# Hawk and stick-breaking trunk, one core: output projection with residual pieces spread out, one root chain for two token tiles, and another order of its last products

## The reference

```python
h = _rmsnorm(x, a_norm);  proj = h @ a_w_in               # layer 0: recurrent branch and gate, 2560 wide
x = x + (y * silu(gate)) @ a_w_out                        # y: conv, block-diagonal gates, RG-LRU scan
k, v = _rmsnorm(x, kv_norm) @ w_kv                        # shared keys and values
q, gate = _rmsnorm(x, b_norm) @ b_w_in                    # layer 1
o = _stick_breaking_attention(q, k, v)                    # 16 heads of 128
x = x + (o * silu(gate)) @ b_w_out                        # the stage that the change is in
return _rmsnorm(x, final_norm)                            # x * rsqrt(mean(x*x) + 1e-6) * gain
```

## Time and profile before

| | |
|---|---|
| median of three runs | 1665.99 us |
| the profiled execution | 1664.41 us |
| its span, first to last instruction | 1662.7 us |
| granted TensorE clock, mean | 0.998 of full speed |
| PE busy | 1641.9 us, 99% |
| DVE, ACT busy | 1133.9 us (68%), 866.3 us (52%) |
| last matmul starts at | 1650.41 us |

### The profile page before, as it was taken

One profiled execution on the slowest core, in us unless ns is written; L12 is line 12 of the kernel. 1 busy time (PEld: TensorE's weight loads), 2 busy tenths in 40 slices (PEclk: granted clock), 3 DMA queues, 4 the chain that ended last, 5 costly groups with the idle time before them and its releaser, 6 DMA issues. The chain is left out here.

```text
span 1662.7 us, 24345 instructions
## 1 busy us (share of the span) xinstructions
PE 1641.9 (99%) x7479; PEld 1363.8 (82%) x7479; DVE 1133.9 (68%) x1988; ACT 866.3 (52%) x1711; POOL 225.8 (14%) x221
## 2 busy tenths in 40 slices
PE   9999999999999999999999999999999999999997
PEld 8888888888888888888888888888888888887785
DVE  5788887778775545478564666675757666678767
ACT  7655566665565333356555544454554444455555
POOL 0121212122121313120000111011110111010000
PEclk9999999999999999999999999999999999999999
DMA  5556555665433343347666544536353545558765
GB/s 188 176 179 201 167 164 174 202 196 183 146 99 95 105 121 107 119 134 223 206 219 181 166 145 150 188 122 196 114 188 112 187 141 159 173 172 291 248 235 185
DMA packets 216839, 280.81 MB, mean 169 GB/s; under 512 B 16488, under 2 KB 145720, under 8 KB 216760
## 3 DMA queue, kind: packets, MB, share of 16 engines
q1 hardware_dynamic: 212152, 270.05, 51.1%
q10 hardware_dynamic: 4608, 9.83, 1.8%
HBM read 229.09 MB, written 50.72 MB: 168 GB/s over the span
## 5 line engine op out<-in xcount | busy, mean ns | idle before, releaser
L726 PE MATMUL ps<-x_hi,w_hi 128*128 128x512 f32 x1408 | 551.0, 391 | 0.0
L726 PE MATMUL ps<-x_hi,w_lo 128*128 128x512 f32 x1408 | 548.4, 389 | 0.0
L726 PE MATMUL ps<-x_lo,w_hi 128*128 128x512 f32 x1408 | 548.2, 389 | 0.0
L1524 DVE SCALAR_TENSOR_TENSOR w_lo<-stage,cT,w_hi 128x256 fp32r<-128x256 f32 x352 | 192.3, 546 | 284.9 <-ACT w_hi L1064 283.6
L1062 ACT ACTIVATE w_hi<-stage,cT 128x256 fp32r<-128x256 f32 x352 | 178.7, 508 | 374.0 <-PE ps L726 350.0
L726 PEld LDWEIGHTS ps<-x_hi,w_lo 128*128 128x128 f32 x1408 | 264.3, 188 | 55.2
L726 PEld LDWEIGHTS ps<-x_hi,w_hi 128*128 128x128 f32 x1408 | 264.4, 188 | 53.8 <-issue 0.4
L726 PEld LDWEIGHTS ps<-x_lo,w_hi 128*128 128x128 f32 x1408 | 264.4, 188 | 53.7 <-issue 0.2
L1064 ACT ACTIVATE w_hi<-stage,cT 128x256 fp32r<-128x256 f32 x352 | 174.5, 496 | 0.0
L1526 DVE SCALAR_TENSOR_TENSOR w_lo<-stage,cT,w_hi 128x256 fp32r<-128x256 f32 x352 | 172.4, 490 | 0.0
L1521 DVE TENSOR_TENSOR w_lo<-stage,w_hi 128x512 fp32r<-128x512 f32 x100 | 86.9, 869 | 116.5 <-ACT w_hi L1060 116.5
(11 more groups left out here) (253 smaller groups left out, 2579.4 us busy)
## 6 DMA issues: line engine op xcount, KB each, us to landing
stage<-in_a_w_in SPq DMA_DIRECT2D x160, 256.0 KB, 2.8
stage<-in_b_w_in SPq DMA_DIRECT2D x128, 256.0 KB, 2.8
stage<-in_w_kv SPq DMA_DIRECT2D x95, 256.0 KB, 3.0
stage<-in_a_w_out SPq DMA_DIRECT2D x80, 256.0 KB, 2.6
b_raw<-in_w_kv SPq DMA_DIRECT2D x64, 256.0 KB, 3.9
t_scratch<-b_raw SPq DMA_DIRECT2D x64, 256.0 KB, 3.6
wb<-in_b_w_out SPq DMA_DIRECT2D x64, 256.0 KB, 4.7
wt_scratch<-wb SPq DMA_DIRECT2D x64, 256.0 KB, 3.3
```

Source lines behind the costliest of these rows:

```text
L726: mm = pe.matmul(dst, a, b, start=start and n == 0, stop=stop and n == 2, skip_group_check=not check)
L1524: nc.vector.scalar_tensor_tensor(w_lo[:, slot, 0:256], stage[:, slot, 0:256], cT[:, col:col + 1], f(w_hi[:, slot, 0:256]), ALU.mult, ALU.s ...
```

## The change

In `out_operand`: q = 1 and q = 2 change places (p1's second part before p6's first). Three operands, not two, are pulled ahead of p6's last part in each group. In group 1 the order after p5 is p2 parts 0 and 1, p4 parts 0 to 7, p2 parts 2 to 7, p3, where it was p2, p4, p3.

The residual's loads and additions get other places: the `uo` copy and sum go from steps 20 and 21 to 23 and 24 (plus 56 in group 1), the six additions of `uo` from steps 26 to 31 to steps 31, 32, 41, 42, 45, 47, and the first eight loads of `x1t_scratch` to later steps. At the end c21 (from p4) is made at step 103 and its squares are taken after step 106; c11 (from p2) goes behind the norm of tiles 2 and 3, which have one root chain together.

```diff
-OUT_LAST = 2
+OUT_LAST = 3
 def out_operand(q):
     g, o = divmod(q, NO)
     late = 2 * VP - 1
+    if q in (1, 2):
+        return operand(3 - q)
...
     if g == VG - 1 and o >= 4 * VP:
-        return g, (o - 4 * VP) % VP, ("p2", "p4", "p3")[(o - 4 * VP) // VP]
+        n = o - 4 * VP
+        if n >= 2 * VP:
+            return g, n - 2 * VP, "p3"
+        return (g, n, "p2") if n < 2 else (g, n - 2, "p4") if n < VP + 2 else (g, n - VP, "p2")
...
-X1T_IN = {26: (2, 1), 27: (3, 1), 28: (2, 0), 29: (3, 0), 31: (0, 1), 32: (1, 1), 44: (0, 0), 46: (1, 0),
+X1T_IN = {27: (2, 1), 29: (3, 1), 37: (2, 0), 38: (3, 0), 40: (0, 1), 41: (1, 1), 50: (0, 0), 52: (1, 0),
...
+U_AT = 2 * VP + AHEAD_V + 3
+U_ADD = {31: 0, 32: 1, 41: 2, 42: 3, 45: 4, 47: 5}
 # ACT, out_step
-                if o == 2 * VP + AHEAD_V - 1:
+                if o == U_AT - 1:
...
-                if q == OUT_RING - 1:
-                    squares(c11o_ready, g, 0, 2 * g)
+                if q == OUT_RING + 2:
+                    squares(c21o_ready, g, 2, 2 * g)
 # ACT, the end
-            squares(c21o_ready, g, 2, 2 * g)
-            for n, t in enumerate((2, 3)):
-                finish(n, t)
-            for n, t in enumerate((0, 1)):
-                square(c12o_ready, g, t, 0, 2 * g + 1)
-                finish(2 + n, t)
+            root_of(3, slice(2, 4))
+            scale(3, 2)
+            scale(3, 3)
+            squares(c11o_ready, g, 0, 2 * g)
+            square(c12o_ready, g, 0, 0, 2 * g + 1)
+            root_of(4, slice(0, 1))
+            scale(4, 0)
+            square(c12o_ready, g, 1, 0, 2 * g + 1)
+            root_of(5, slice(1, 2))
+            scale(5, 1)
 # DVE, out_step
-                if o == 2 * VP + AHEAD_V:
+                if o == U_AT:
...
-                    if o == 2 * VP + AHEAD_V + 5 + e:
+                    if U_ADD.get(o) == e:
...
-                if q == OUT_RING - VP + AHEAD_V:
-                    make_c11(g)
-                for e, (t, c) in enumerate(((2, 3), (3, 3), (0, 2), (1, 2))):
+                if q == OUT_OPERAND[VG - 1, VP - 1, "p4"] + 1 + AHEAD_V:
+                    make_c21(g)
+                for e, (t, c) in enumerate(((2, 3), (3, 3))):
                     if q == VOPS - 4 + e:
 # DVE, the end
-            make_c21(g)
-            for n, t in enumerate((2, 3)):
-                finish(n, t, 14)
-            for n, t in enumerate((0, 1)):
-                make_c12(g, t)
-                finish(2 + n, t, 15 + t)
+            root_of(3, slice(2, 4), 12)
+            dve.wait_ge(gained, 2)
+            scale(2)
+            scale(3)
+            make_c11(g)
+            for t in (0, 1):
+                gain(t, 2, 14)
+            make_c12(g, 0)
+            root_of(4, slice(0, 1), 15)
+            dve.wait_ge(gained, 4)
+            scale(0)
+            make_c12(g, 1)
+            root_of(5, slice(1, 2), 16)
+            scale(1)
```

More of the change, by code:

```diff
@@ L142 @@
 OY_IN = {23: 0, 25: 1, 30: 2, 33: 3, 36: 4, 39: 5, 42: 6}
-X1T_IN = {26: (2, 1), 27: (3, 1), 28: (2, 0), 29: (3, 0), 31: (0, 1), 32: (1, 1), 44: (0, 0), 46: (1, 0),
+X1T_IN = {27: (2, 1), 29: (3, 1), 37: (2, 0), 38: (3, 0), 40: (0, 1), 41: (1, 1), 50: (0, 0), 52: (1, 0),
           58: (2, 3), 60: (3, 3), 62: (2, 2), 64: (3, 2), 66: (0, 3), 68: (1, 3), 70: (0, 2), 72: (1, 2)}
-X1T_GROUP = {26: 0, 27: 0, 28: 1, 29: 1, 31: 1, 32: 1, 44: 2, 46: 2}
+X1T_GROUP = {27: 0, 29: 0, 37: 1, 38: 1, 40: 1, 41: 1, 50: 2, 52: 2}
+U_AT = 2 * VP + AHEAD_V + 3
+U_ADD = {31: 0, 32: 1, 41: 2, 42: 3, 45: 4, 47: 5}
 GAIN_IN = {76: 0, 80: 1}
@@ L1487, in _, with root_of, scale @@
             g = VG - 1
-            squares(c21o_ready, g, 2, 2 * g)
[L1490 to L1495, removed]
+            def root_of(nth, one):
+                act.wait_ge(sqrt_in, nth)
+                nc.scalar.activation(small[:, 1, one], small[:, 1, one], ACT.Sqrt).then_inc(sqrt_out, 1)
+            def scale(nth, t):
+                act.wait_ge(rs_ready, nth)
+                act.wait_ge(gained, 2)
                 nc.scalar.activation(x2[:, t, 0:D // 2], x2[:, t, 0:D // 2], ACT.Identity,
                                      scale=rs_tok[:, t:t + 1]).then_inc(scaled_a, 1)
-            for n, t in enumerate((2, 3)):
-                finish(n, t)
-            for n, t in enumerate((0, 1)):
-                square(c12o_ready, g, t, 0, 2 * g + 1)
-                finish(2 + n, t)
+            root_of(3, slice(2, 4))
[8 more added lines that the diff above has]
+            scale(5, 1)
         @block.vector
@@ L1999, in out_step, with gain @@
                     nc.vector.tensor_tensor(x, x, g_fin[:, 512 * c:512 * c + 512], ALU.mult)
-                if q == OUT_RING - VP + AHEAD_V:
-                    make_c11(g)
-                for e, (t, c) in enumerate(((2, 3), (3, 3), (0, 2), (1, 2))):
+                if q == OUT_OPERAND[VG - 1, VP - 1, "p4"] + 1 + AHEAD_V:
+                    make_c21(g)
+                for e, (t, c) in enumerate(((2, 3), (3, 3))):
                     if q == VOPS - 4 + e:
-                        dve.wait_ge(x2_sq, 10 if c == 3 else 12)
-                        x = x2[:, t, 512 * c:512 * c + 512]
-                        nc.vector.tensor_tensor(x, x, g_fin[:, 512 * c:512 * c + 512], ALU.mult).then_inc(gained, 1)
+                        gain(t, c, 10)
+            def gain(t, c, squared):
+                dve.wait_ge(x2_sq, squared)
+                x = x2[:, t, 512 * c:512 * c + 512]
+                nc.vector.tensor_tensor(x, x, g_fin[:, 512 * c:512 * c + 512], ALU.mult).then_inc(gained, 1)
             GAIN_AT = {2 * VP + 12 + 2 * n: (n % 4, n // 4) for n in range(8)}
@@ L2066, in _, with root_of, scale @@
             g = VG - 1
-            make_c21(g)
-            def finish(n, t, squared):
-                one = slice(t, t + 1)
+            def root_of(nth, one, squared):
                 dve.wait_ge(x2_sq, squared)
[L2073 to L2076, removed]
+                link(nc.vector.tensor_reduce(ss[:, one], ss5[:, one, 0:4], AX.X, ALU.add))
+                rsqrt(ss[:, one], small[:, 0, one], small[:, 1, one], small[:, 2, one], rs_tok[:, one], nth)
+            def scale(t):
                 done, last = ((3, 2), (2, 3))[t < 2]
```

## The result

The changed kernel has a median of 1657.65 us (1656.87 to 1659.85, six runs) against 1666.03 us before (1665.73 to 1666.95, six runs): ratio 0.995, 95% interval 0.9937 to 0.9963, 8.4 us less. The forecast was 1658.8. The profiled execution took 1657.79 us with a span of 1656.1 us.

What follows compares the result with a forecast made beforehand. PE's waits for DVE and ACT, then the tail on DVE and ACT, bound the kernel. 1.36 + 0.4 + 3.7 + 1.7 = 7.2 us off 1664.41 gave 1657.2, plus 1.6 to the median: 1658.8, range 1656.8 to 1662.8.

Steps and rivals of the forecast that it cites:

- The exchange: PE's second product: swapping q = 1 and 2 removes the wait for g_taken, gain 1.36 us, passed on.
- The third pulled operand: PE at q = 17: p6's last part comes later, so its wait for DVE goes; gain 0.4 us.
- The stretch from q = 29 to 34: PE waits on late DVE and ACT work: 5.4 us lost, 1.6 to stay, 3.7 taken as gain.
- ACT standing for DMA between steps 31 and 38: Sign on ACT's timeline: any such wait there would show the forecast wrong; no size given.
- A: Rival, 17%: moved residual loads make weights late again, the 3.7 us gain falls to 0.5; time 1662.0 us.
- The last group's order: Group 1 on PE: p4's first part at q = 90 waits for nothing; cost 0 with 1.0 us of cover.
- The tail: After the last low parts, on DVE and ACT: tile 0's make_c12 starts at 1648.25, not 1649.99; gain 1.7 us.
- drain of about 1380 ns: ACT's table load in the tail: with this drain the tail gains 0.9 us, not 1.7; time 1659.6 us.
- The step from the traces to the medians: Whole kernel: 1.6 us added because the runs' median was that much above the profiled execution.
- B: Rival, 10%: DVE's scans for the last head pair set the pace, early 1.36 and 0.4 us lost; 1660.6 us.
- D: Rival, 4%, slower: DVE's addition at step 41 waits for residual loads, needing a 25.5 us landing; 1669.3 us.

Runs made afterwards that it cites:

- the end alone: Kernel before with only the last group's new order, c21 at step 103 and the single root chain; 1663.21 us, ratio 0.9984.
- swap_undone: Changed kernel with q = 1 and q = 2 back in the old order; 1659.10 us.
- combined: Changed kernel, tile 0's make_c12 before the gains, p4 and p3 one product later in group 0, p6's first part before p1's in group 1; 1655.46 us.

## Why the prediction was right

The time came out 1.15 us under the forecast and inside its range, faster as forecast. Step by step:

- The exchange, 1.36 us. Right in size: 1.43 us lost before, 0.07 after, 1.45 by the medians when taken out. What the prediction lacked is the condition: on top of the end alone, without the spreading, the exchange and the third pulled operand gave nothing. I priced each gain of PE as if it stood by itself.
- The third pulled operand, 0.4 us. In every kernel that has it the 0.30 us at q = 17 and the slow matmul are gone. It had no run of its own.
- The stretch from q = 29 to 34, 3.7 us: 5.5 us were lost with the slow matmuls, 1.6 are, 3.9 gained. What I left standing, 0.2 and 1.4, was measured as 0.27 and 1.21 with 0.07 and 0.08 behind. The wrong part is the sharing out. I named the copy, the loads and the additions as three causes, and took the additions on DVE to be as good as the whole wait at q = 33. The copy alone gives 1.9 of the spreading's 4.0 us by the traces and 2.5 of 4.7 by the medians, and put back last it costs 4.4; the loads make 1.0 us of q = 33, and the additions 1.3 in one trace and 0.1, which is unclear, by the medians. I also missed that the additions at their old steps wait for the residual's loads themselves (0.81 and 1.24 us in two traces).
- ACT standing for DMA between steps 31 and 38 was one of the four signs that were to show the forecast wrong, and it came: ACT stood 1.52 us at step 31, 1.05 and 1.00 at 38 and 39. It cost 0.1 us at most (q = 33 lost 0.27 us here and 0.18 in swap_undone, where ACT didn't stand at step 31), so the sign was badly chosen. A's mechanism was there, and its price wasn't; "combined" shows what it costs when it falls on step 36.
- The last group's order, 0. Right: PE has no row with idle time in group 1 behind its first product.
- The tail, 1.7 us: 1.78. The root chain starts 9.46 us before the last matmul (9.4 forecast), c11's additions 5.72 us before it, and each piece of the sum came within 0.1 us: chain 1.61 for 1.57, scalings 2.13 for 2.14, squares 2.28 for 2.28. The Trainium skill's drain of about 1380 ns with a table load ("ScalarE: Activation LUTs", section "What ACT_TABLE_LOAD costs") would have put the square root behind 1637.4 if it follows the load; it began at 1636.72, when DVE released it. The forecast from rows held, that from the page didn't.
- The step from the traces to the medians. The sum off the profiled execution's time was 7.2 and the traces show 7.5. The term that was mis-sized is the 1.6 us added from the profiled execution to the median: the changed kernel's median lies 0.1 us under its profiled execution. That makes 1.7 us too much, of which 0.9 were made up by the unchanged part, longer in this trace; with 0.3 too little in the sum this is the 1.15. Part of the closeness is luck, as two of these errors have opposite signs. Why the kernel before usually runs at a lower mean clock than its profiled execution did stays open.

B expected the early gain to be given back; the trace of the exchange alone gives it back, in the kernel without the spreading, and to late weights, not to the scans. D asked for a landing of 25.5 us; the median was 5.0.

## What to carry to other kernels

Where one engine's queue feeds the loads, look first for an instruction in it that waits for the far end of the pipeline: a copy placed three steps too early, where it had to wait for PE, held up the weights' high parts, through them the low parts, through them the loads, and was worth about as much as the loads and additions spread around it. Price a gain on the bound engine together with what that engine runs into next; an edit that shows nothing may be worth its full size once the next wait is gone. When two waits in a row are a chain on another engine, put one piece of other work ahead of them; the chain itself can stay where it is.

## What the runs showed of the hardware

After a wait at q = 33 of 2.80 and 2.82 us the matmuls of one product came 0.43 us apart and not 0.227 in two of the traces (the exchange alone, and the spreading undone). In the former the stretches show, with the granted clock as the column behind POOL's:

```profile
1540.00:1543.00 3.00, 0.65 (x3) 0.19 (x1) 3.00 (x6) 2.25 (x4) 0.00 (x0) 0.98 0.76 234
1543.00:1546.00 3.00, 2.55 (x6) 1.82 (x6) 3.00 (x6) 0.00 (x0) 0.00 (x0) 0.50 1.00 364
1546.00:1549.00 3.00, 3.00 (x13) 2.45 (x13) 1.31 (x3) 2.46 (x7) 0.00 (x0) 0.95 0.68 234
```

That is the lower level, 1.2 GHz: shorter stretches place its start at about 1542.95 us, while PE still waited, and its end at about 1546.3, 2.8 us behind the start of q = 33. The two executions have a mean granted clock of 0.996 and 0.997. The kernel before waited as long, 2.79 us, and kept 1.00, and so did the end alone, with 1.26 us lost at q = 29 as well; what sets the two apart stays open. The slow product takes 1.2 us more and then finds q = 34's data ready, so little is lost by it here: q = 34 starts 2.70 us behind q = 33 and not 2.66. It did not occur in the trace of the changed kernel, whose longest wait here is 1.05 us.
